# A phasor table built once, the state-space setup split between two engines, and each chunk spread over two retention heads

## What is computed

```python
dt = exp(log_dt)                                     # per group
mag = exp(lam_re * dt)
ab_re, ab_im = mag * cos(lam_im * dt), mag * sin(lam_im * dt)
f_re = ((ab_re - 1) * lam_re + ab_im * lam_im) / den # den = lam_re**2 + lam_im**2
f_im = (ab_im * lam_re - (ab_re - 1) * lam_im) / den
bb = f * B                                           # complex, per state
bu = einsum('bsgh,gph->sbgp', u, bb)                 # complex
x = associative_scan(x[t] = ab * x[t-1] + bu[t])     # over 256 tokens
y = einsum('sbgp,ghp->bsgh', x_re, c_re) - einsum(x_im, c_im)
y = gelu(y + d_skip * u); y = y * sigmoid(y @ glu_w + glu_b)
```

## Time and profile before

| what | value |
|---|---|
| median of three runs | 2258.28 us (2257.92 to 2261.22) |
| profiled execution, its own time | 2257.0 us |
| its span in the trace | 2255.2 us |
| PE busy in the span | 2162.7 us, 96% |
| DVE, ACT, POOL busy | 1471.7, 1003.2, 776.3 us |
| mixer of the even layer up to its output projection | 0 to 438.6 us of the span |

### The profile page before, as it was taken

One profiled execution on the slowest core, in us unless ns is written; L12 is line 12 of the kernel. 1 busy time (PEld: TensorE's weight loads), 2 busy tenths in 40 slices (PEclk: granted clock), 3 DMA queues, 4 the chain that ended last, 5 costly groups with the idle time before them and its releaser, 6 DMA issues.

```text
span 2255.2 us, 47390 instructions
## 1 busy us (share of the span) xinstructions
PE 2162.7 (96%) x18426; PEld 2132.9 (95%) x18426; DVE 1471.7 (65%) x1747; ACT 1003.2 (44%) x1244; POOL 776.3 (34%) x880
## 2 busy tenths in 40 slices
PE   8788888999999999999999999999999999999997
PEld 8788777999999999999999989999999999999997
DVE  6378766577666655666666666677666555666666
ACT  4243333444444444444444445545444444444442
POOL 5799995023434300433411000023443101443311
PEclk9899998999999999999999999999999999999999
DMA  6334233454555456555455533455554556554553
GB/s 262 114 135 154 98 135 125 158 201 178 207 200 187 166 193 221 196 194 186 176 187 198 192 125 123 162 192 188 206 187 174 186 193 220 197 187 185 174 197 114
DMA packets 64604, 398.69 MB, mean 177 GB/s; under 512 B 7169, under 2 KB 9729, under 8 KB 29057
## 3 DMA queue, kind: packets, MB, share of 16 engines
q1 hardware_dynamic: 60192, 391.15, 48.2%
q10 hardware_dynamic: 4320, 6.27, 0.8%
HBM read 395.29 MB, written 2.10 MB: 176 GB/s over the span
## 4 chain that ended last, share of the span: by engine, by line
PE 81%; POOLq 9%; POOL 5%; issue 2%; DVE 2%; ACT 1%; DVEq 0%; DMA 0%; ACTq 0%
PE PS L1401 25%; PE PS L1402 25%; PE PS L1405 25%; POOLq L1288 2%; POOLq L1292 2%; POOL g L1290 2%; POOL E L1293 2%; POOLq L1159 2%; POOLq L1166 1%; PE PS L1396 1%; PE PS L1397 1%; PE PS L1398 1%; POOLq L1306 1%; POOL S L1305 1%; PE PS L1751 0%
## 5 line engine op out<-in xcount | busy, mean ns | idle before, releaser
L705 DVE TENSOR_TENSOR lo<-raw,hi 128x1024 fp32r<-128x1024 f32 (+2 forms) x826 | 950.4, 1170 | 527.0 <-ACT hi L356 521.8
L356 ACT ACTIVATE hi<-raw 128x1024 fp32r<-128x1024 f32 (+2 forms) x826 | 785.8, 969 | 722.2 <-PE PS L1405 676.1
L1401 PE MATMUL PS<-XS,hi 128*128 128x256 f32 x3584 | 851.6, 280 | 8.2 <-ACT hi L356 8.2
L1402 PE MATMUL PS<-XS,hi 128*128 128x256 f32 x3584 | 845.4, 278 | 0.0
L1401 PEld LDWEIGHTS PS<-XS,hi 128*128 128x128 f32 x3584 | 680.2, 190 | 15.8 <-issue 15.4
L1402 PEld LDWEIGHTS PS<-XS,hi 128*128 128x128 f32 x3584 | 680.4, 190 | 0.4
L1405 PE MATMUL PS<-XS,lo 128*128 128x256 f32 x3584 | 480.8, 277 | 0.0
L1405 PEld LDWEIGHTS PS<-XS,lo 128*128 128x128 f32 x3584 | 441.5, 188 | 0.0
L1401 PE MATMUL PS<-YF,hi 128*128 128x256 f32 x1408 | 331.8, 276 | 0.0
L1402 PE MATMUL PS<-YF,hi 128*128 128x256 f32 x1408 | 331.8, 276 | 0.0
L1358 POOL TENSOR_TENSOR ctmp<-apad,cws 128x512 f32<-128x512 f32 x88 | 131.9, 1519 | 526.0 <-DVE apad L756 526.0
(11 more groups left out here) (238 smaller groups left out, 2487.7 us busy)
## 6 DMA issues: line engine op xcount, KB each, us to landing
raw<-in_ffn_up SPq DMA_DIRECT2D x176, 1024.0 KB, 4.8
raw<-in_ffn_dn SPq DMA_DIRECT2D x128, 704.0 KB, 4.1
raw<-in_w_in SPq DMA_DIRECT2D x51, 1024.0 KB, 4.9
raw<-in_w_oe SPq DMA_DIRECT2D x16, 1024.0 KB, 4.8
raw<-in_w_oo SPq DMA_DIRECT2D x16, 1024.0 KB, 4.8
raw<-in_mla_dn SPq DMA_DIRECT2D x9, 1024.0 KB, 4.8
raw<-in_w_ukv SPq DMA_DIRECT2D x8, 1024.0 KB, 4.8
raw<-in_w_uq SPq DMA_DIRECT2D x8, 768.0 KB, 4.3
```

Source lines behind the costliest of these rows:

```text
L356: act.activation(hi[:, p % SLOTS, 0:n], raw[:, u % SLOTS, off:off + n], ACT.Copy).then_inc(hi_ready, 1)
L705: V.tensor_tensor(lo[:, p % SLOTS, 0:n], raw[:, u % SLOTS, off:off + n], f(hi[:, p % SLOTS, 0:n]), ALU.subtract).then_inc(lo_ready, 1)
L1401: mm(PS[:, bank, 0:T], wh, x[:, 0:T], start=first, stop=False)
L1402: mm(PS[:, bank, 0:T], wh, x[:, T:2 * T], start=False, stop=False)
```

## The change

`E32`, a table of the first 32 phasors of all 16 columns, is made once after the setup (`first_phasors`, five levels on POOL). It takes the place of `acc` and `lot`, which are idle then. `phasors` copies its two columns from the table and does levels 5 to 7 only.

The setup is split. POOL does dt, theta and mag (`s5_magnitude`, then `th_ready`) without waiting for DVE's reciprocal. DVE does cosine and sine (`s5_angles`, 18 operations) after its pieces of Q in head 0, the first phasor (`s5_phasor`, 16 operations, then `ph_ready`) between the second and third pieces of V, the factor (`s5_factor`, 11) between the second and third pieces of G, and f * B (`s5_b`, 6 operations on 128x512) after `Pm` of head 0. POOL does the powers (`s5_powers`) once `ph_ready` is there.

A chunk now reaches into the next head. `b_u(0)` to `b_u(3)` stand after K's second and third piece, V's second and third; `c_x(0)` stays in V; `c_x(1)` moves from the end of G to after the second K piece of the next head, and `scan(1)` from before DVE's first G-step piece to after the third. `scan(0)` moves back by one piece. `y5` moves to the next head. POOL rotates the first half before it negates `Cst`. The core of the diff:

```diff
-        phst = sb("phst", [P, 8, 2, 2], fp32, even)
+        phst = sb("phst", [P, 3, 2, 2], fp32, even)
+        acc, lot = sums[:, 0:2, :], sums[:, 2:4, :]
+        E32 = sums[:, :, :].rearrange("p a t -> p (a t)").rearrange("p (a m n) -> p a m n", a=2, m=KD)
@@ ACT, even_head
-                if s5:
-                    if h0 > 1:
-                        act.wait_ge(c_done, S_(0, 2))
-                    act.dma_start(Cst[:, :, :, :].rearrange("p a b c -> p (a b c)"),
                 for i in range(4):
                     if h0 == 0 or i:
                         split(p0 + 4 + i, 16, r)
                     if s5 and i == 1:
                         bu_copy(0)
+                        load_c()
+                    if s5 and i == 2:
+                        bu_copy(1)
+                    if glu and i == 1:
+                        act.wait_ge(c_done, 8)
+                        act.dma_start(gluw, A["gluw"]).then_inc(gluw_in, 16)
-                for i in range(4):
-                    split(p0 + 8 + i, 16, r)
-                    if s5 and i == 0:
-                        bu_copy(1)
+                splits(p0 + 8, 16, r)
                 for i in range(4):
                     split(p0 + 12 + i, 16, r)
-                    if s5 and i < 2:
-                        bu_copy(i + 2)
+                    if s5 and i in (1, 2):
+                        bu_copy(i + 1)
@@ DVE
+            def s5_b():
+                B, o, w = (x.rearrange("p a b t -> p (a b t)").rearrange("p (a m c) -> p a m c", a=2, m=KD)
+                           for x in (sB, sT1, sT2))
+                fr, fi = (col(i).unsqueeze(2).broadcast_to([P, KD, 32]) for i in (10, 11))
+                tt(o[:, 0], B[:, 0], fr, ALU.mult)
+                tt(w[:, 0], B[:, 1], fi, ALU.mult)
+                tt(o[:, 0], o[:, 0], w[:, 0], ALU.subtract)
+                tt(o[:, 1], B[:, 1], fr, ALU.mult)
+                tt(w[:, 0], B[:, 0], fi, ALU.mult)
+                V.tensor_tensor(o[:, 1], o[:, 1], w[:, 0], ALU.add).then_inc(bb_ready, 1)
                 for i in range(4):
                     if h0 == 0 or i:
                         split(p0 + 4 + i, 16, r)
+                    if h0 > 1 and i == 2:
+                        y5()
+                if h0 == 0:
+                    s5_angles()
                 rotate(KRo, p0 + 4, e0)
                 for i in range(4):
                     split(p0 + 8 + i, 16, r)
-                    if s5 and i == 1:
+                    if s5 and i == 2:
                         scan(0)
+                    if h0 == 0 and i == 1:
+                        s5_phasor()
                 rotate(QRo, p0 + 8, e0 + 1)
-                splits(p0 + 12, 16, r)
+                for i in range(4):
+                    split(p0 + 12 + i, 16, r)
+                    if h0 == 0 and i == 1:
+                        s5_factor()
-                if s5:
-                    scan(1)
+                if h0 == 0:
+                    s5_b()
                 for i in range(4):
                     split(p0 + 16 + i, 16, r)
+                    if s5 and i == 2:
+                        scan(1)
@@ POOL
+            def s5_powers():
+                a, b = col(20), col(21)
+                pool.wait_ge(ph_ready, 1)
+            def first_phasors():
+                G.memset(E32[:, 0, :, 0:1], 1.0)
+                G.memset(E32[:, 1, :, 0:1], 0.0)
+                for l in range(5):
+                    n = 1 << l
             def phasors(k, h0, r):
-                for l in range(8):
+                G.tensor_copy(e[:, :, :, 0:32], E32[:, :, m:m + 2, :] if r is None else E32[:, :, ds(r * 4 + m, 2), :])
+                for l in range(5, 8):
@@ PE
                 def after_k(i):
-                    if s5 and i == 1:
-                        b_u(0)
+                    if h0 > 1 and i == 1:
+                        c_x(1)
+                    if s5 and i in (1, 2):
+                        b_u(i - 1)
-                    if s5:
-                        if i == 1:
-                            c_x(0)
-                            b_u(3)
+                    if s5 and i == 1:
+                        c_x(0)
+                        b_u(2)
+                    if s5 and i == 2:
+                        b_u(3)
```

More of the change, by code:

```diff
@@ L34 @@
 EPS = 1e-6
+MAGIC = 12582912.0
 SLOTS = 4
@@ L787, in lambda_squared, with tt, ts @@
                 dve.drain()
-                V.reciprocal(pt[:, 12, :], pt[:, 13, :]).then_inc(den_ready, 1)
+                V.reciprocal(pt[:, 12, :], pt[:, 13, :])
+            def tt(o, a, b, op):
+                V.tensor_tensor(o, a, b, op)
+                dve.drain()
+            def ts(o, a, s1, s2, o1, o2=None):
+                if o2 is None:
+                    V.tensor_scalar(o, a, s1, None, o1)
+                else:
+                    V.tensor_scalar(o, a, s1, s2, o1, o2)
+                dve.drain()
@@ new lines, in stt, with s5_angles @@
+            def stt(o, a, s, b, o1, o2):
+                V.scalar_tensor_tensor(out=o, in0=a, scalar=s, in1=b, op0=o1, op1=o2)
+                dve.drain()
+            def s5_angles():
+                th, cs, sn, a, b, c = (col(i) for i in (2, 3, 4, 5, 6, 7))
+                dve.wait_ge(th_ready, 1)
+                ts(a, th, 2.0 / math.pi, MAGIC, ALU.mult, ALU.add)
+                ts(a, a, -MAGIC, None, ALU.add)
+                parts, rest = [], math.pi / 2
+                for bits in (8, 9, 10):
+                    scale = 2.0 ** (bits - 1 - math.floor(math.log2(rest)))
+                    v = math.floor(rest * scale) / scale
+                    parts.append(v)
+                    rest -= v
+                parts.append(rest)
+                stt(b, a, -parts[0], th, ALU.mult, ALU.add)
+                for v in parts[1:]:
+                    stt(b, a, -v, b, ALU.mult, ALU.add)
+                tt(c, b, b, ALU.mult)
+                ts(sn, c, 1.0 / 362880, None, ALU.mult)
+                for k in (-5040, 120, -6):
+                    stt(sn, sn, 1.0 / k, c, ALU.add, ALU.mult)
+                stt(sn, sn, 1.0, b, ALU.add, ALU.mult)
+                ts(cs, c, -1.0 / 3628800, None, ALU.mult)
+                for k in (40320, -720, 24, -2):
+                    stt(cs, cs, 1.0 / k, c, ALU.add, ALU.mult)
+                ts(cs, cs, 1.0, None, ALU.add)
@@ new lines, in s5_phasor @@
+            def s5_phasor():
+                cs, sn, a, b, c, d_, e_, g_ = (col(i) for i in (3, 4, 5, 6, 7, 8, 9, 10))
+                ts(b, a, 0.25, MAGIC, ALU.mult, ALU.add)
+                ts(b, b, -MAGIC, None, ALU.add)
+                stt(a, b, -4.0, a, ALU.mult, ALU.add)
+                ts(b, a, 0.0, None, ALU.is_equal)
+                tt(c, a, a, ALU.mult)
+                ts(c, c, 4.0, None, ALU.is_equal)
+                tt(b, b, c, ALU.subtract)
+                ts(c, a, 1.0, None, ALU.is_equal)
+                ts(d_, a, -1.0, None, ALU.is_equal)
+                tt(c, c, d_, ALU.subtract)
+                tt(d_, cs, b, ALU.mult)
+                tt(e_, sn, c, ALU.mult)
+                tt(ph[:, 0, 0, :], d_, e_, ALU.subtract)
+                tt(e_, sn, b, ALU.mult)
+                tt(g_, cs, c, ALU.mult)
+                V.tensor_tensor(ph[:, 0, 1, :], e_, g_, ALU.add).then_inc(ph_ready, 1)
+                dve.drain()
@@ new lines, in s5_factor @@
+            def s5_factor():
+                lre, lim = (vec[:, VEC[k]:VEC[k] + KD] for k in ("lre", "lim"))
+                a, b, g_, h_, c = (col(i) for i in (5, 6, 10, 11, 12))
+                tt(a, mag[:, :], ph[:, 0, 0, :], ALU.mult)
+                ts(a, a, -1.0, None, ALU.add)
+                tt(b, mag[:, :], ph[:, 0, 1, :], ALU.mult)
+                tt(g_, a, lre, ALU.mult)
+                tt(h_, b, lim, ALU.mult)
+                tt(g_, g_, h_, ALU.add)
+                tt(g_, g_, c, ALU.mult)
+                tt(h_, b, lre, ALU.mult)
+                tt(b, a, lim, ALU.mult)
+                tt(h_, h_, b, ALU.subtract)
+                tt(h_, h_, c, ALU.mult)
@@ L1141, in sum_squares @@
                 pool.wait_ge(sum_done, n)
+                pool.drain()
                 G.memset(acc[:, :, :], 0.0)
```

180 lines of the change are left out of this document (63 added, 117 removed).

## The result

The changed kernel takes 2264.89 us (median of 20 runs, 2259.59 to 2269.35), the kernel before 2257.69 us (median of 20 runs beside them, 2255.92 to 2263.26). The ratio is 1.003, with a 95% interval from 1.0023 to 1.0038: slower by 0.3%, where 1.4% less was forecast. The profiled execution of the changed kernel took 2260.95 us.

What follows compares the result with a forecast made beforehand. POOL was taken to pace heads 1 to 4 and its setup the end of head 0. Output projection at 406.3 instead of 438.6 saves 32.3 us: 2257.0 to 2224.7, median 2226.0; range 2205 to 2243.

Steps and rivals of the forecast that it cites:

- Head 0: Setup moved partly to DVE: transposes wait 1.5 us, head done at 93.4 in place of 108.46, a gain of 15.1.
- PE's own work per head: PE's matmuls in one head without waits: 54.8 us, of which sixteen pieces take 45.3 and nine small things 9.5.
- POOL's chunk: POOL's work per head without the first doubling levels: from 68.4 to some 44 us, so POOL no longer paces a head.
- The new wait at `b_u(1)`: In heads 2 to 4 PE waits 6.4 us for ACT's first copy, which stands behind `YE`.
- Head 5: Last of the heads forecast: 64.6 us, with waits of 1.2 and 2.6 and 0.7 of half clock.
- what is late next: Paragraph following one period of the changed kernel: 54.8 work, 6.4 and 1.0 waits, 2.5 half clock, 64.7 us in all.
- so `c_x(1)` need not wait: At the C product after K's second piece: `scan(1)` ends at 8.9 us, PE arrives at 9.5.
- Rival 2: DVE held by POOL's rotation during the K rotation, 2 to 4 us a head plus 5 in head 0: 2242; chance 0.20.
- no larger sum follows from it than the rival below prices: The DVE and POOL shared-port lock costs no more than the DVE-held-by-POOL rival's 13 to 19 us lost.
- The half clock: PE running at 1.2 GHz behind the `b_u(1)` wait: 2.5 us a head, uncertain from 0 to 2.5.
- Rival 3: TensorE stays at 1.2 GHz after the new wait, 1.6 us per further piece, up to 2276; chance 0.04.
- Head 1: Stretch to G's last piece: 54.2 us, with 2.6 waiting at `b_u(1)`; POOL's lateness at `b_u(0)` covered by that wait.

Runs made afterwards that it cites:

- e5: The changed kernel with one more wait: POOL builds a pair's phasors only after DVE's scan before it has ended; 2238.7 us.
- e8: The changed kernel with the first chunk's operands staged before the phasor table instead of behind it; 2264.4 us.
- e9: e5 with the first chunk's operands staged before the phasor table; 2237.9 us.
- e6: The kernel before with the split setup alone, order of heads and full phasors as before; 2243.9 us.
- e11: e10 with the first chunk staged before the table and `scan(1)` behind the first low part of the next step; 2238.3 us.
- e2: The changed kernel without the table: all eight phasor levels built as before, split setup and new order kept; 2238.0 us.
- e3: The changed kernel with table and split setup, but the order of the heads of the kernel before on all engines; 2227.1 us.
- e10: e3 with `c_x(0)` and `b_u(3)` after V's third piece and `scan(0)` after the third V low part; 2227.6 us.

## Why the prediction was wrong

By the marks of the two profiled executions the forecast of 2224.7 us missed 2260.95 by 36.3: head 0 -2.2, head 1 +12.6, heads 2 to 4 +27.3, head 5 -2.6, behind it +1.2.

**Right.** Head 0: the transposes do not wait at all (1.5 was put), done at 91.24 against 93.4. PE's own work per head, 54.8: 54.7 in the changed kernel and 54.5 to 55.8 in all without fillers. POOL's chunk, 44: 41.35 busy. The new wait at `b_u(1)` for ACT's copy: 4.44 in the changed kernel and 6.89 in e5, forecast 6.4; its chain from the scan's end to the second B u took 11.1 us and in e5 12.0, forecast 12.0. Head 5: 61.95 for 64.6.

**The step that failed** is in the paragraph on what is late next: "`scan(1)` starts at about 2.4 and ends 6.48 later", and from it "so `c_x(1)` need not wait". The 6.48 came from a trace in which POOL stood at copies and tiny levels beside the scan, and the forecast itself took those levels away. It had weighed how much POOL has to do ("so POOL no longer paces a head") and not when it does what is left: with 26 us of small levels gone the large ones start at once, under the scans. From there the terms fell one after the other. The scan started at 3.4 and took 8.9, so `c_x(1)`, said not to wait, waited 3.16; `scan(0)`, given a wait of 1.0, took 9.2 and waited 3.56. e5 shows the cause: with one wait that moves POOL's phasors behind the scan, 26 us come back.

**Rival 2** had the right two engines and the wrong place and price: it put the meeting on the K rotation at 2 to 4 us a head. In the period shown, the halves of that rotation took 0.43 and 0.42 us, where the earlier trace rows has 2.61: there was no meeting there. (Its sum is off too: 4 us in each of four heads and 5 make 21, not 19.) The forecast said of the Trainium skill's lock (SBUF — State Buffer, "Who interferes with whom") that "no larger sum follows from it than the rival below prices". A larger one did. The Trainium skill has it there that a DVE operation with two inputs in SBUF and a GpSimd operation that reads there cannot run together; the trace agrees in kind (a scan operation of 0.66 us took up to 1.46 beside POOL operations of 0.9 to 1.4). What it came to, over two scans and what follows each, was 2.4 and 2.7 us of longer scans in a head, and the waits behind them.

**The half clock**, the term of the period with the largest miss, was charged once a head, "at 2.5 as after the long waits". There were three waits, and each cost it: after 3.16 us the piece took 4.4, after 4.44 it took 5.5, after 3.56 the B u 2.07 and the piece 5.0. That is 8.5 us a head in the mean where 2.5 were put, so 6.0 of the 9.1 us by which the period (73.8) is over the forecast (64.7); 3.2 are idle time. Of the 7.2 us by which a period is longer than in e5, 5.1 are half clock and 2.5 idle time. Rival 3, a clock that stays low for five pieces or more, did not occur: behind each wait the product or B u and one piece were slow, and of the next piece little (3.17 us at the most).

**Head 1**, "54.2": 66.75 in the changed kernel, 62.6 in e5. The forecast took POOL's lateness at the first B u as "close, but the next wait covers it". POOL's table was done at 103.55, where "ready at 94 to 102" was put, and the two copies behind it, done at 105.7, had no term; PE, which came 2.4 us earlier than forecast, waited 8.03 there, and the half clock followed. What counts more, POOL's chain on to the first rotation had no term at all. e8 and e9 show that this chain, not the staging, is the bound.

Of the miss of 38.9 us (2226.0 to 2264.9) e5 accounts for 26.2, by medians. (The two executions that the traces show lie only 19.4 apart, 2260.95 and 2241.59: the first is the second shortest of its kernel's 20, the second the longest of its four. At the output projection they are 22.8 apart.) The other 12.7 are, by the marks of e5 against the forecast's, head 1 with +8.4 and the three periods with +5.7, less 1.3 in head 0 and 0.5 in head 5. This second split is read and not made by an edit. Open is what would shorten head 1, which none of the kernels with an edit brought under the 62.0 us of e6 (57.0 before), and which of its two edits costs e11 its 10.7 us.

## What to carry to other kernels

Before taking work off an engine, lay its remaining operations on the time axis where they will then fall, and ask what runs beside them on an engine that it is seen to slow down: here the small levels had been a useful delay, and one wait, no work removed, was worth 26 us. A duration read from a trace holds for what ran beside it in that trace; if the change moves that, the duration is no longer known. Two edits that each win can lose together (16.8 us and a less sure 5.9 won apart, 21.0 lost as a pair), so time them apart and as a pair. And count TensorE's waits by number too: three of 3 to 4.5 us cost as much idle time as the one long and one short wait they replace, and nearly three times the half clock.

## What the runs showed of the hardware

- VectorE's scans beside GpSimd's 128x256 and 128x512 operations: 1.05 us each in the median over 100 to 240 us in the changed kernel (up to 1.46), 0.66 with GpSimd waiting (e5) or at levels of up to 32 elements (e2, up to 0.88).
- It goes the other way too: in e2 GpSimd's operations on 128x8 took 1.23 and 1.18 us while VectorE was in its two of 128x1024 (157.91 and 159.05), and two of that size only 0.20 and 0.21 at 163.16 and 163.32. So part of the 13 us that the five small levels cost was time beside VectorE.
- TensorE's clock fell to 1.2 GHz behind waits of 3.16, 3.56 and 4.44 us as it did behind 8.73, for part or all of the piece that followed (mean granted 0.65, 0.57 and 0.50, and 0.61). Behind 3.16 us the C product still ran at full clock (1.06 us) and the fall came in the B u after it. Behind 1.23 us (e5) the next pieces ran at 2.4 GHz. Between them it went both ways: behind 1.97 us (before) and 2.29 us (e3, head 1) nothing was slow; behind 2.09 us (e10) the C product took 1.93 instead of 1.06; behind 2.19 us (changed kernel, head 3) the B u ran at full clock and the piece after it took 4.6 us.
- GpSimd's rotation (128x1024) took 3.4 us an operation where VectorE was at work on low parts beside it and 2.4 to 2.6 elsewhere (e3), and the low parts up to 3.41 instead of 1.2: both sides are slowed.
